# One RWKV stage of a hybrid decoder layer: products on halves of the array, half-width level products, and a loop written out

## The reference, cut to what matters

```python
def wkv7_scan(S0, r, w, k, v, a, b):
    def step(S, inp):
        r_t, w_t, k_t, v_t, a_t, b_t = inp
        Sa = jnp.einsum('bhvk,bhk->bhv', S, a_t)
        S = S * w_t[:, :, None, :] + Sa[..., None] * b_t[:, :, None, :] + v_t[..., None] * k_t[:, :, None, :]
        y = jnp.einsum('bhvk,bhk->bhv', S, r_t)
        return S, y
```

## Time and profile before

| what | value |
|---|---|
| median of 3 runs | 4152.35 us (4150.67 to 4154.87) |
| span of the profiled execution | 4145.3 us |
| of it the RWKV stage | 979 us (2184 to 3163) |
| PE busy in the RWKV stage | 913.6 us |
| DVE / ACT / POOL busy there | 668.3 / 303.1 / 298.2 us |
| mean granted PE clock there | 0.96 of full speed |

### The profile page before, as it was taken

The page is one execution under the profiler, slowest core; times in us unless marked ns, Lnnn a source line. Parts: engine busy times, 40 slices in busy tenths (PEclk is TensorE's granted clock), DMA queues, the critical chain, the costliest instruction groups (busy, mean ns, idle before and its releaser), DMA issues. The chain is left out here.

```text
span 4145.3 us, 59925 instructions
## 1 busy us (share of the span) xinstructions
PE 3927.6 (95%) x26462; PEld 3802.6 (92%) x26462; DVE 1452.6 (35%) x1723; ACT 459.1 (11%) x655; POOL 421.4 (10%) x300
## 2 busy tenths in 40 slices
PE   8999999999999999999996999999996699979994
PEld 7999999999999999999995888888885599979994
DVE  5121122112112112112116776777753733341123
ACT  2000000000000000000002333333322410020000
POOL 0000000000000000000003333333323200002110
PEclk9999999999999999999998999999997799999997
DMA  4112112112111111111102111111114433343225
GB/s 158 63 65 75 62 62 78 62 62 77 63 62 74 66 62 69 71 62 68 72 32 60 27 28 25 25 28 28 28 35 164 158 127 110 116 171 108 84 73 210
DMA packets 153965, 318.17 MB, mean 77 GB/s; under 512 B 98928, under 2 KB 99200, under 8 KB 140032
## 3 DMA queue, kind: packets, MB, share of 16 engines
q1 hardware_dynamic: 108816, 206.91, 15.2%
q10 hardware_dynamic: 44464, 108.51, 7.0%
q0 software_dynamic: 576, 1.08, 0.1%
HBM read 227.51 MB, written 88.96 MB: 76 GB/s over the span
## 5 line engine op out<-in xcount | busy, mean ns | idle before, releaser
L171 PE MATMUL in_acc<-in_xh,in_wh 128*128 128x364 f32 x4272 | 948.7, 330 | 1.7 <-issue 1.7
L171 PE MATMUL in_acc<-in_xl,in_wh 128*128 128x364 f32 x4272 | 941.7, 328 | 0.0
L171 PE MATMUL in_acc<-in_xh,in_wl 128*128 128x364 f32 x4272 | 941.5, 328 | 0.0
L171 PEld LDWEIGHTS in_acc<-in_xh,in_wh 128*128 128x128 f32 x4272 | 744.0, 188 | 6.0 <-issue 2.5
L171 PEld LDWEIGHTS in_acc<-in_xl,in_wh 128*128 128x128 f32 x4272 | 742.5, 188 | 0.0
L171 PEld LDWEIGHTS in_acc<-in_xh,in_wl 128*128 128x128 f32 x4272 | 740.7, 188 | 0.0
L310 DVE TENSOR_TENSOR in_stage<-in_acc,in_rstd 128x1092 f32<-128x1092 f32 x89 | 115.3, 1296 | 1689.2 <-PE in_acc L171 1689.1
L517 ACT ACT_TABLE_LOAD x17 | 21.8, 1283 | 2129.5 <-DVE mix L502 2129.2
L1132 POOL MEMSET gn_eps<- 128x1 f32 x1 | 0.1, 98 | 2182.6 <-POOLq L126 2182.6
L159 DVE TENSOR_TENSOR in_wl<-in_raw,in_wh 128x2048 fp32r<-128x2048 f32 x89 | 204.0, 2292 | 3.0
L171 PE MATMUL out_acc<-out_xh,out_wh 128*128 128x364 f32 x768 | 171.6, 332 | 22.0 <-DVE out_xl L1445 20.4
(11 more groups left out here) (220 smaller groups left out, 4160.3 us busy)
## 6 DMA issues: line engine op xcount, KB each, us to landing
in_raw<-in_w_in SPq DMA_DIRECT2D x89, 1024.0 KB, 4.8
z<-in_stage ACTq DMA_DIRECT2D x89, 548.0 KB, 2.7
mg_gate<-z SPq DMA_DIRECT2D x32, 546.0 KB, 3.6
mg_raw<-in_w_proj SPq DMA_DIRECT2D x32, 512.0 KB, 4.8
out_raw<-in_w_out SPq DMA_DIRECT2D x16, 1024.0 KB, 5.0
zin<-z SPq DMA_DIRECT2D x17, 812.5 KB, 5.5
mT<-mg_out ACTq DMA_DIRECT2D x16, 546.0 KB, 6.1
hT<-out_xs ACTq DMA_DIRECT2D x16, 546.0 KB, 3.4
```

What stands on the lines that cost most here:

```text
L171: mm = pe.matmul(self.acc[s][:, c, 0:NCH], w[s][:, k * P:(k + 1) * P], x[:, kx, c * NCH:(c + 1) * NCH], start=(k == 0 and w is self.wh and ...
```

## The change

Six things, all inside `phase_rwkv`:

1. **Level products**: `half_of` gives the half of the columns that is used, and L754, L762 and L765 move 64 columns instead of 128. The weights stay 128 x 128. DVE reads the result compactly.
2. **Products per head on halves of the array**: `t_rhs`, `t_u`, `t_m` and `t_lowrank` use the 64 rows of one head as contraction (both heads alternate, pair by pair), and `t_state` and `t_y` put out the 64 rows of one head, alternating too. Two heads go to different PSUM banks or partition halves.
3. The number of products: `t_lowrank` 8 to 16, `t_m` 8 to 16 (with 128 moving columns instead of 256), `t_state` 8 to 16 (64 weight columns and 64 moving ones instead of 128 and 128); `t_rhs`, `t_u` and `t_y` keep theirs.
4. **DVE**: `v_state` is one instruction on 128 x 512 instead of four on 64 x 256; `v_ar` is three instead of four; the masks read other banks.
5. **ACT**: `a_rhs` is two copies on 64 x 512 instead of four on 64 x 256; both copies of `a_rhs` and of `a_u` now wait for the end of the whole product, where they used to start after the first half; `a_sample_x` is eight small copies instead of two.
6. **The loop is written out**: all 17 steps stand one after another, with constants in the waits.

```diff
+        def half_of(ap, b, side):
+            return ap.rearrange("p (n h b) -> p n h b", h=2, b=b)[:, :, side, :]
+        def compact(n, b):
+            return bank[n][:, H4].rearrange("p (n b) -> p n b", b=b)
...
         def t_lowrank(pe, c):
-                for p in range(4 * f, 4 * f + 4):
-                    mm = pe.matmul(by(EE[f], 4)[:, p % 4, :], lrw[:, p * P:(p + 1) * P],
-                                   lr[:, :, :].rearrange("p j c -> p (j c)"), start=True, stop=True)
+            for p in range(PAIRS):
+                for j in range(2):
+                    mm = pe.matmul(by(EE[j], PAIRS)[:, p, :], lrw[H2[j], p * P:(p + 1) * P], lr[H2[j], :],
+                                   start=True, stop=True)
...
         def v_ar(dve, c, part):
-            dve.scalar_tensor_tensor(a[H2[h], :, h, 0, :], kk[H2[h], :, :], -1.0, em[H2[h], :, :],
-                                     MUL, MUL).then_inc(ar_ready, 1)
-            dve.tensor_tensor(a[H2[h], :, h, 1, :], r[H2[h], :, :], ep[H2[h], :, :], MUL).then_inc(ar_ready, 1)
+            if part == 0:
+                dve.scalar_tensor_tensor(a[:, :, 1, :], kk[:, :, :], -1.0, em[:, :, :], MUL, MUL).then_inc(ar_ready, 1)
+            else:
+                for h in range(2):
+                    dve.tensor_tensor(a[H2[h], :, 2 * h, :], r[H2[h], :, :], ep[H2[h], :, :], MUL).then_inc(ar_ready, 1)
...
         def t_m(pe, c):
-                for p in (2 * q, 2 * q + 1):
-                    mm = pe.matmul(bank[MM[q]][:, (p % 2) * 256:(p % 2) * 256 + 256],
-                                   bk[:, p, :, :].rearrange("p j c -> p (j c)"),
-                                   a[:, p, :, :, :].rearrange("p h j c -> p (h j c)"), start=True, stop=True)
+            for p in range(PAIRS):
+                for h in range(2):
+                    mm = pe.matmul(by(MM[p // 4 * 2 + h], 4)[:, p % 4, :], bk[H2[h], p, :, :].rearrange("p j c -> p (j c)"),
+                                   a[H2[h], p, h:h + 2, :].rearrange("p j c -> p (j c)"), start=True, stop=True)
...
         def t_level(pe, c, n):
-                    mm = pe.matmul(by(LL[f], 4)[:, p % 4, :], at[:, p, :], t[:, p, :], start=True, stop=True)
+                    mm = pe.matmul(by(LL[f], PAIRS)[:, p % 4, :], at[:, p, :], half_of(t[:, p, :], b, 0),
+                                   start=True, stop=True)
...
         def t_rhs(pe, c):
-                for p in range(4 * f, 4 * f + 4):
-                    for h in range(2):
-                        out = by(BB[f], 4)[H2[0], p % 4, H2[h]]
-                            pe.matmul(out, a[:, p, h, 0, :], st[:, p, :], start=True, stop=False)
-                        mm = pe.matmul(out, mc[:, p, h, 0, :], zc[:, p, H2[h]], start=False, stop=True)
+            for p in range(PAIRS):
+                for h in range(2):
+                    out = by(BB[h], PAIRS)[H2[h], p, :]
+                        pe.matmul(out, a[H2[h], p, 1, :], st[H2[h], p, :], start=(p == 0), stop=False)
+            for p in range(PAIRS):
+                for h in range(2):
+                    mm = pe.matmul(by(BB[h], PAIRS)[H2[h], p, :], mc[:, p, h, A_AT[h], :], zc[:, p, H2[h]], start=False,
+                                   stop=(p == PAIRS - 1))
...
         def t_u(pe, c):
-                        mm = pe.matmul(by(BB[f], 4)[H2[0], p % 4, H2[h]], pb(tt, c)[:, p, H2[h]], xst[:, p, :],
-                                       start=True, stop=True)
+                    mm = pe.matmul(by(BB[h], PAIRS)[H2[0], p, :], pb(tt, c)[H2[h], p, H2[h]], xst[H2[h], p, :],
+                                   start=True, stop=True)
...
         def t_state(pe, c):
-                        mm = pe.matmul(by(BB[f], 4)[:, p % 4, :], pb(bkt, c)[:, p, :],
-                                       (zmask[b % 2] if sample else pb(zz, c))[:, p, :], start=True, stop=True)
+                    for h in range(2):
+                        mm = pe.matmul(by(BB[b % 2], PAIRS)[H2[h], p, :], pb(bkt, c)[:, p, H2[h]],
+                                       (zmask[b % 2] if sample else pb(zz, c))[:, p, H2[h]], start=True, stop=True)
...
         def v_state(dve, c):
-                    for h in range(2):
-                        dve.tensor_tensor(dst[H2[h], FOUR[f], :], stw[H2[h], FOUR[f], :],
-                                          by(BB[f], 4)[H2[h], :, H2[h]], ADD).then_inc(st_ready, 1)
+                dve.tensor_tensor(dst, stw[:, :, :], by(BB[b % 2], PAIRS), ADD).then_inc(st_ready, 1)
...
         def all_steps(engine, step):
-            with engine.Fori(1, (NCHUNK - 2) // 2) as j:
-                for odd in range(2):
-                    c, e, d = j * 2 + odd, j * 2 + (odd + 1), j * 2 + (odd - 1)
-                    step(engine, c, e, d)
+            for c in range(SMP + 1):
+                step(engine, c, c + 1 if c < SMP else None, c - 1 if c else None)
```

More of the change, by code:

```diff
@@ L57 @@
 NH = 2 * PAIRS
-TABLES = {"ident": P, "avg": P, "ones": P, "diag2": P, "mask": 2 * CH, "sample_mask": 2 * CH, "hsum": PAIRS * NH,
+TABLES = {"ident": P, "avg": P, "ones": P, "diag2": P, "mask": 3 * CH, "sample_mask": 3 * CH, "hsum": PAIRS * NH,
           "of_pair": PAIRS, "to_head": P, "reset": PAIRS * CH, "sample_reset": PAIRS * CH,
@@ L447, in is_sample @@
         def is_sample(c):
-            return isinstance(c, int) and c == SMP
+            return c == SMP
         def halves_of(ap, b):
@@ L791, in t_rhs @@
         def t_rhs(pe, c):
             sample, a, mc, zc = is_sample(c), pb(ar, c), pb(m, c), pb(zz, c)
-            after(pe, st_ready, c * 4)
+            after(pe, st_ready, c)
             after(pe, yn_ready, c)
-            for f in range(2):
-                if sample:
-                    pe.wait_ge(xr_ready, f + 1)
-                for p in range(4 * f, 4 * f + 4):
-                    for h in range(2):
-                        out = by(BB[f], 4)[H2[0], p % 4, H2[h]]
-                        if sample:
-                            pe.matmul(out, xr[:, p, 0, :], ident[:, H2[h]], start=True, stop=False)
-                        else:
-                            pe.matmul(out, a[:, p, h, 0, :], st[:, p, :], start=True, stop=False)
-                        mm = pe.matmul(out, mc[:, p, h, 0, :], zc[:, p, H2[h]], start=False, stop=True)
-                mm.then_inc(x_done, 1)
@@ L809, in a_rhs @@
[L809 to L824 removed]
+            if sample:
+                pe.wait_ge(xr_ready, 8)
@@ new lines, in t_rhs @@
+            for p in range(PAIRS):
+                for h in range(2):
+                    out = by(BB[h], PAIRS)[H2[h], p, :]
+                    if sample:
+                        pe.matmul(out, xr[:, p, 0, :], ident[:, H2[h]], start=(p == 0), stop=False)
+                    else:
+                        pe.matmul(out, a[H2[h], p, 1, :], st[H2[h], p, :], start=(p == 0), stop=False)
[3 more added lines that the diff above has]
+                                   stop=(p == PAIRS - 1))
+                    if p == PAIRS - 1:
+                        mm.then_inc(x_done, 1)
@@ new lines, in a_rhs, with t_u @@
+        def a_rhs(act, c):
+            for h in range(2):
+                act.wait_ge(x_done, c * 2 + h + 1)
+                nc.scalar.activation(xst[H2[h], :, :], by(BB[h], PAIRS)[H2[h], :, :], ACT.Copy).then_inc(x_ready, 1)
+        def t_u(pe, c):
+            pe.wait_ge(x_ready, c * 2 + 2)
+            for p in range(PAIRS):
+                for h in range(2):
+                    mm = pe.matmul(by(BB[h], PAIRS)[H2[0], p, :], pb(tt, c)[H2[h], p, H2[h]], xst[H2[h], p, :],
+                                   start=True, stop=True)
+                    if p == PAIRS - 1:
+                        mm.then_inc(u_done, 1)
@@ L1116, in _ @@
                     sp.dma_start(dst, src).then_inc(par_loaded, 16)
-                with sp.Fori(1, NCHUNK) as c:
+                for c in range(1, SMP + 1):
                     sync_load(sp, c)
-                sync_load(sp, SMP)
                 sp.dma_start(sts[:, :, :, :], stateT).then_inc(sts_loaded, 16)
```

161 lines of the change are left out of this document (74 added, 87 removed).

## The result

The changed kernel takes **4351.26 us** (median of 4 runs, 4347.89 to 4370.53) against 4153.61 for the kernel before on the same chip: a ratio of 1.0484 [1.0463, 1.0506]. It is 198 us slower where 74 us faster was forecast, and lies far outside the range of 4056 to 4130.

A forecast was written before the change was run, and what follows sets the result against it. PE's list plus a few short waits was taken to bound a chunk. Savings of 52.5 (15 x 3.5), loop 8, chunk 0 1.5, chunk 16 3.5 and sample 8.5 sum to 74 us: 4078.4 us, range 4056 to 4130.

The forecast's parts named there:

- Level products at price nothing: Half-wide level products on PE: 224 passes a chunk keep 0.112 us each, so 0 gained.
- The load bound: Level products on PE: loading 128 weight columns takes about 107 ns and sets the pass time, not the moving columns.
- The falling clock as a rival: Half-clock piece in every chunk, 1.5 us lost, like the chunk at 2529.15; 4102 us, 18% shared with partial overlap.
- Two halves at once: Products on array halves overlap fully on PE: 0.029 us a pass at 64 by 64, 0.056 at 128 weight columns.
- The three rivals on overlap: Only column halves overlap, 4126 us, 8%; only row halves, 4121, 3%; nothing overlaps in a sustained stream, 4182, 6%.
- The wait before `t_u`: PE waits 2 to 3 us for ACT's `xst`, itself behind the store; `t_u` starts at V+7.85.
- V: Start of `t_values`, taken as zero of a chunk; times in us count from it.
- DVE's chain: Fourth score mask to first level mask: 9.0 us of unchanged DVE work, mask at V+15.2, 2.8 us gained a chunk.
- Loop: Writing out the RWKV stage's loop removes all 8 us lost at its turns.
- Sample: State updates after chunk 16 take about 1.4 us a sequence instead of 2.54, saving 8.5 us in all.

The follow-up runs named there:

- e1: The changed kernel with all level products moving the full 128 columns again: 4105.0 us.
- e4: e1 with the store of y issued one step later on ACT and POOL's scaling held until DVE finishes the low-rank columns: 4065.2 us.
- e3: The kernel before with only the loop of the RWKV stage written out: 4143.6 us.
- g2: e4 with POOL's gate and bonus products moved behind its scaling product: 4038.3 us.
- h1: The kernel before with only half-wide level products, plus two extra DVE products behind `tt` whose results nobody reads: 4252.5 us.
- i1: The changed kernel with `t_lowrank` and its readers as in the kernel before: 4163.5 us.
- f3: The changed kernel with only the first level's products half-wide, the other four levels full: 4200.4 us.
- h2: The changed kernel with POOL's scaling one step later and its gate and bonus products behind it, the store left in place: 4097.1 us.
- f1: The changed kernel, half-wide levels kept, with the store of y and POOL's scaling each one step later: 4092.9 us.
- g1: e1 with POOL's gate and bonus products moved behind its scaling product: 4096.5 us.

## Why the prediction was wrong, point by point

- **Level products at price nothing: right in time, and the step that failed all the same.** At full clock their sixteen passes take 1.8 us as before; at half clock 3.5 (L762 in the kernel after, 2786.25 to 2789.72). The load bound holds. But I priced them only in passes and asked nothing about the clock that such a stream is granted. The bounds I gave, 0 and a gain of 12 us a chunk, excluded a loss with no reason from a row. It was the clock that went: net of all gains 25.3 us were lost in chunk 0 and 181.7 in the next fifteen, and full-wide levels (e1) take the whole kernel from 4351 to 4105.
- **The falling clock as a rival was there, but sized wrongly.** I took one piece like that of 2529.15 in each chunk, 1.5 us lost, and 4102. The chunk shown has 27.3 us at 1.2 GHz and is 10.9 longer than e1's. I assumed that a fallen clock comes back by itself. The earlier trace rows bore on that: there PE was busy without a gap with half-size work, 64 columns of weights and 16 moving, and the clock stayed at 0.50 for 20 us. I read this row for the load's price and not for what it says of the clock.
- **Two halves at once: right.** `t_m` takes 2.0 us (1.8 and a change of shape), the 64 passes of the rhs 2.16, `t_y` 1.9 (e4: 2413.57 to 2415.5), in all chunks at full clock. The three rivals on overlap are out.
- **The wait before `t_u`: right,** 2.18 us on ACT's `xst`; `t_u` began at V+7.6 (forecast V+7.85), and in e1 the level at V+13.3 (V+13.65). Behind it the clock is low for 3.4 us only; it is not what starts the long stretch.
- **DVE's chain: mis-sized.** "Nothing in that is changed" left out POOL. The first level mask begins at V+16.9 in e1, not V+15.2: the two additions into `at` meet POOL's gate and bonus products and take 1.6 us longer. So PE waits 2.08 us there where 0.4 was forecast, and the period is 50.9, not 49.5. Fifteen periods of e1 take 767.6 us against the 742.6 forecast. That is 25 of the 27 us by which its median misses; its profiled span misses by 33, and most of the other 8 lie behind the last state update, in work that the change leaves alone. The same delay of DVE lengthens the wait behind which the clock falls in the kernel after, so the small error may have had a part in the large one; the kernel after with this delay alone removed was not run.
- **Loop: right,** 8.7 us for 8 (e3).
- **Sample: right.** DVE in e1:

```profile
3094.05 0.69 DVE L902 TENSOR_TENSOR sts<-stw,bank 128x512 f32<-128x512 f32 x1 [1.11 <-PE bank L881]
...
3104.19 0.69 DVE L902 TENSOR_TENSOR sts<-stw,bank 128x512 f32<-128x512 f32 x1
```

The last seven sequences take 10.14 us, 1.45 each (forecast 1.4, before 2.54). From the start of chunk 16 to the last state update e1 needs 74.5 us where the kernel before needed 86.4: 11.9 for the 12 of the forecast.

So the arithmetic of the change was sound for the kernel with full-wide levels, up to one term on DVE. What broke it is that a part which looked free left light work around a wait, and there the clock fell and stayed down.

## What to carry to other kernels

Before halving a product whose time is set by its weight load, ask what it gives back in time; if nothing, leave it full, for its columns may be what keeps the clock at 2.4 GHz over the next wait. A row in which a busy PE sits at 0.50 is evidence about light work, and belongs to the bounds of every edit that makes work lighter. When one engine's chain is moved earlier, check whom it now runs beside: moving three products on POOL and the store on ACT, none of them on PE's list, was worth 67 us (e1 to g2), all of the change but its loop and its half-wide levels 39 (e3 to e1).

## What the runs showed of the hardware that was not expected

- **The clock can fall in the middle of work and then stay low while PE is busy.** A window of the kernel after, in the chunk ahead of the one shown, has PE busy for all of its 23.9 us, at 0.50, that is 1.2 GHz, and the next at full clock:

```profile
2714.40:2738.30 23.90, 23.90 (x153) 22.20 (x152) 10.77 (x18) 6.83 (x10) 6.60 (x5) 0.50 0.19 35
2738.40:2757.00 18.60, 18.38 (x150) 16.14 (x149) 12.89 (x28) 0.94 (x2) 0.00 (x0) 1.00 0.00 1
```

  In the chunks shown, full-wide work preceded the rise: 512 moving columns (L903, after), 128x128 products with 128 rows (L535 in h1, L532 in i1, L774 in f3). It is no sure cure: in the stretches of 64.9 us L903, L612, L618 and L934, all with 512 moving columns, pass at 1.2 GHz, and the clock rises only in the next chunk's rhs products, behind the transposes L653. Half-wide products right behind a fall did not lift it, yet they held the full clock where no wait stood among them (h2, f1). In i1 the clock rose in low-rank products half of which are zeros.
- **DVE beside POOL.** Two additions of 64x512 took 2.99 us beside POOL's products and 1.40 alone; a 128x64 product 1.22 (g1) against 0.23 (e1); a 128x64 tensor-scalar instruction 2.85 against 0.25 (e1 and e4), about as long as POOL's 2.76 us product next to it. The score masks, which read one operand from a bank, follow each other at 0.62 us beside POOL's `bkw` product (2625.50 to 2627.6 in e1), so none took more than the 0.69 that all 68 of them took in the kernel before. The Trainium skill, "SBUF — State Buffer", Who interferes with whom, says that a DVE instruction with two inputs in SBUF contends with a GpSimd instruction that reads SBUF; the rows of `at` and of the 128x64 product agree, and I had not asked it of `at`. The tensor-scalar instruction reads one tile only and is not what that sentence speaks of.
